# A two-layer gated-recurrence and attention block: who copies the keys of a new head pair into the working place

## What is computed

```python
q, i_in, f_fw, f_bw, z = jnp.split(h @ w_in, 5, axis=-1)
k_d = (1.0 - lbd) * jax.nn.sigmoid(-g_d)       # keys, for d = forward, backward
f_d = lbd + (1 - lbd) * jax.nn.sigmoid(g_d)    # forget gates (lbd is 0 for a single layer)
# chunk by chunk, per head:
o_inter = (q * cumulative_f) @ S
scores  = sum_k q[t] * decay[t, s] * k[s]
S_new   = diag(f_total) * S + (k * decay).T @ v
# then o = o_forward + o_backward, an RMS norm over each head, times silu(z), times w_out
```

## Time and profile before

| | |
|---|---|
| median of 3 runs | 2602.09 us (2599.35 to 2602.85) |
| the profiled execution itself | 2599.4 us, of which the span of the engines is 2597.6 us |
| TensorE busy | 2508.6 us, 97% of the span |
| VectorE, ScalarE, GpSimd busy | 1203.8, 608.2 and 263.4 us |
| mean granted TensorE clock | 0.99 of full |

### The profile page before, as it was taken

The page is one execution under the profiler, slowest core; times in us unless marked ns, Lnnn a source line. Parts: engine busy times, 40 slices in busy tenths (PEclk is TensorE's granted clock), DMA queues, the critical chain, the costliest instruction groups (busy, mean ns, idle before and its releaser), DMA issues.

```text
span 2597.6 us, 33413 instructions
## 1 busy us (share of the span) xinstructions
PE 2508.6 (97%) x13400; PEld 1959.5 (75%) x13400; DVE 1203.8 (46%) x2083; ACT 608.2 (23%) x1202; POOL 263.4 (10%) x194
## 2 busy tenths in 40 slices
PE   7999999999999999899999999999999999999999
PEld 3688888888887587666886444788886687889998
DVE  3277686696696412344136111146664014115961
ACT  3132323233232121233225100121111023113211
POOL 0012111111021100000000000111220000003310
PEclk9999999999999999999999999999999999999999
DMA  9453343343433223112520222322342232354562
GB/s 354 161 179 130 113 161 132 126 145 114 140 119 114 90 64 114 47 40 75 142 69 1 65 65 65 98 81 82 85 122 67 67 81 65 98 176 132 163 180 64
DMA packets 320030, 284.83 MB, mean 110 GB/s; under 512 B 27649, under 2 KB 298633, under 8 KB 319545
## 3 DMA queue, kind: packets, MB, share of 16 engines
q1 hardware_dynamic: 318170, 279.08, 34.7%
q0 software_dynamic: 1280, 4.20, 0.4%
q10 hardware_dynamic: 479, 0.13, 0.0%
HBM read 280.24 MB, written 3.15 MB: 109 GB/s over the span
## 4 chain that ended last, share of the span: by engine, by line
PE 82%; DVE 11%; issue 3%; ACT 3%; DMA 1%; SPq 0%; DVEq 0%; ACTq 0%
PE ps L1358 11%; PE ps L1287 10%; PE ps L721 8%; PE ps L1437 4%; PE ps L781 4%; PE ps L1425 4%; PE ps L1325 3%; PE ps L1299 3%; PE ps L819 3%; PE ps L772 2%; PE ps L905 2%; PE ps L976 2%; PE ps L925 2%; DVE arena L2317 2%; PE ps L484 2%
## 5 line engine op out<-in xcount | busy, mean ns | idle before, releaser
L1287 PE MATMUL ps<-hT,ring_mem 128*128 128x512 f32 (+1 forms) x768 | 250.3, 486 | 0.0
L1287 PEld LDWEIGHTS ps<-hT,ring_mem 128*128 128x128 f32 x768 | 145.9, 190 | 101.3 <-issue 91.4
L2248 DVE TENSOR_TENSOR arena<-ps,arena 128x512 f32<-128x512 f32 (+1 forms) x48 | 26.8, 558 | 291.2 <-PE ps L1299 291.2
L721 PE MATMUL ps<-xT,ring_mem 128*128 128x256 f32 x672 | 159.3, 380 | 0.1
L721 PE MATMUL ps<-hT,ring_mem 128*128 128x256 f32 x672 | 158.8, 379 | 0.0
L721 PEld LDWEIGHTS ps<-xT,ring_mem 128*128 128x128 f32 x672 | 127.2, 190 | 19.4 <-DVE ring_mem L2014 2.1
L819 PE MATMUL ps<-arena,K_c 128*128 128x128 f32 x896 | 120.6, 289 | 21.0 <-ACT K_c L1630 20.1
L721 PEld LDWEIGHTS ps<-hT,ring_mem 128*128 128x128 f32 x672 | 126.1, 190 | 18.9 <-issue 2.9
L1358 PE MATMUL ps<-hT,arena 128*128 128x256 f32 (+1 forms) x704 | 132.6, 333 | 7.0 <-ACT hT L505 7.0
L819 PEld LDWEIGHTS ps<-arena,K_c 128*128 128x128 f32 x896 | 115.9, 194 | 30.1 <-ACT K_c L1630 12.3
L1358 PE MATMUL ps<-arena 128*128 128x256 f32 (+1 forms) x704 | 130.0, 328 | 0.0
(11 more groups left out here) (307 smaller groups left out, 4334.4 us busy)
## 6 DMA issues: line engine op xcount, KB each, us to landing
ring_mem<-in_w_mod_dram SPq DMA_DIRECT2D x24, 2048.0 KB, 7.6
ring_mem<-in_w_up_dram SPq DMA_DIRECT2D x88, 512.0 KB, 5.1
ring_mem<-in_hg_w_in_dram SPq DMA_DIRECT2D x40, 1024.0 KB, 5.2
ring_mem<-in_w_in_dram SPq DMA_DIRECT2D x30, 1024.0 KB, 5.4
ring_mem<-in_w_down_dram SPq DMA_DIRECT2D x16, 1408.0 KB, 7.1
ring_mem<-in_ada_w_dram SPq DMA_DIRECT2D x8, 2048.0 KB, 7.6
ring_mem<-in_mla_w_in_dram SPq DMA_DIRECT2D x9, 1024.0 KB, 5.3
ring_mem<-in_hg_w_out_dram SPq DMA_DIRECT2D x8, 1024.0 KB, 12.2
```

What stands on the lines that cost most here:

```text
L721: mm = PE.matmul(dst, left[:, k, :], right[:, k, :], start=k == 0, stop=k == 3)
L1287: mm = PE.matmul(ps[:, j, 0:n], wj[:, k, m * 128:m * 128 + 128], hT[:, k, c0:T], start=k == 0, stop=k == 7)
```

## The change

The two copies `Kw <- k_st` leave VectorE and become two ScalarE copies, in a new helper that ScalarE calls behind the squares of each turn, and for pair 0 behind the last of the ten steps, ahead of the loop. A new semaphore `k_kept` counts them. VectorE's `k_sum` now waits for it.

```diff
-        kc_ready = sem("kc_ready")
+        kc_ready, k_kept = sem("kc_ready"), sem("k_kept")
...
+        def hg_unpack_scalar(act, i):
+
+            if not (isinstance(i, int) and i == 0):
+                act.wait_ge(o_full, raised(i * 2))
+            act.wait_ge(act_freed, i * 6 + 4)
+            for d in range(2):
+                S.activation(Kw[:, d * PC:d * PC + PC], k_st[:, 1 - d, :], ACT.Copy).then_inc(k_kept, 1)
...
                 hg_square_scalar(act, i - 1)
+                hg_unpack_scalar(act, i)
                 if more:
                     hg_one_scalar(act, i + 1, 0)
                     hg_seven_scalar(act, i + 1, 0)
                 hg_mean_scalar(act, i - 1)
+            hg_unpack_scalar(act, 0)
             hg_one_scalar(act, 1, 0)
             hg_seven_scalar(act, 1, 0)
...
             V.tensor_tensor(view(Qw, (PC, 2), (1, PC)), view(q_st, (0, 2), (1, PC)), f_st, ALU.mult)
-            V.tensor_copy(Kw[:, 0:PC], k_st[:, 1, :])
-            V.tensor_copy(Kw[:, PC:2 * PC], k_st[:, 0, :])
             if not first:
                 dve.wait_ge(ms_full, i * 2)
+            dve.wait_ge(k_kept, i * 2 + 2)
             V.tensor_tensor(k_sum, k_st[:, 0, :], k_st[:, 1, :], ALU.add).then_inc(unpacked, 1)
```

## The result

The changed kernel takes 2608.14 us (median of 8 runs, 2604.43 to 2612.88), the kernel before 2600.73 us (8 runs, 2599.09 to 2602.85). The ratio is 1.0027, with a 95% interval of 1.0019 to 1.0036: slower by 7.4 us in the medians. The execution that was profiled is one of the quick ones, 2604.5 us with a span of 2602.7 us, against 2599.4 and 2597.6 us in the profile of before.

A forecast was written before the change was run, and what follows sets the result against it. TensorE, 82% of the chain, was taken as the bound, so only its product starts count. Hole +4.5, clock +2.1 and pair 7 -0.4 raise the median from 2602.1 to 2608.3 us; range 2602.5 to 2611.5.

The forecast's parts named there:

- No gain at pairs 1 to 6: Boundaries of pairs 1 to 6: `k_sum` ends some 3.1 us earlier, but nobody takes it up; gain 0.
- Rival 2: Six boundaries: `K_c` comes earlier with `k_sum`, giving back 0.59 us before L819 each; +2.6 in all, 2604.7 us; chance 0.08.
- Gain at pair 7: Pair 7, without next-pair products: TensorE's 0.29 us idle before L816 goes; gain 0.4 us (0.3 to 0.5).
- The hole at the opening: Opening: late ScalarE copies hold `k_sum` and the sums behind it, delaying pair 1's product seven; TensorE hole of 4.5 us.
- The clock behind the hole: TensorE after the opening's hole: granted clock falls to half, costing 2.1 us (1.6 to 2.8).
- Rival 1: Opening: the hole opens but the clock stays at full; +4.1 us, 2606.2 us; chance 0.08.
- Rivals 3 and 4: 3: opening isn't held, -0.4, 2601.7 us, chance 0.07; 4: ScalarE's copies over 3.0 us delay product one, 2611 us, chance 0.05.
- The sum: Whole kernel: hole +4.5, clock +2.1, pair 7 -0.4, so +6.2 us and a median of 2608.3 us, 0.24% slower.
- within 0.2%: Whole kernel: chance 0.32 that the time stays within 0.2% (5.2 us) of the kernel before.

The follow-up runs named there:

- e6_kc_early: Changed kernel with pair 0's copies ahead of the value keeps and each pair's first `K_c` right behind ScalarE's key copies: 2595.62 us, ratio 0.9984 to the kernel before.
- e2: Changed kernel with only its opening kept, VectorE making the copies at the seven boundaries as before: 2607.55 us, ratio 1.0024 to the kernel before.
- e5: Changed kernel with VectorE making pair 1's first two sums ahead of pair 0's unpacking: 2603.87 us, ratio 1.0010 to the kernel before.
- e4: Changed kernel with GpSimd starting its first move only after pair 1's first sums: 2607.97 us, ratio 1.0026 to the kernel before.
- e3b: Changed kernel with ten unread products of 256 columns on TensorE ahead of pair 1's first product: 2607.40 us, ratio 1.0024 to the kernel before.

## Why the prediction was right

The median forecast was 2608.3 us, the measured one 2608.1. The way there was not as exact: the forecast stood on 2602.1 us for the kernel before, from three runs, where eight runs give 2600.7, and on a loss of 6.2 us, where the medians give 7.4. The two errors cancel. The steps, one by one:

- *No gain at pairs 1 to 6*: right. The copies took 2.00 us (forecast 2.1), `k_sum` ended 3.2 us ahead of L816 with nobody waiting, the turns that end at pairs 2 to 6 changed by at most 0.04 us each, and L819's idle time stayed, released by `K_c`. Rival 2 (`K_c` follows `k_sum`) is out. Its price was misread: the 0.59 us were counted at six boundaries, and the old trace has them at four (pairs 2 to 5), 0.72 us at pair 1 released by VectorE (L1960), and none at pair 6, so it could have given back 3.1 us at most. This did not enter the sum. `e6_kc_early` shows from the other side that `K_c` hung on ScalarE's own order.
- *Gain at pair 7*: right in place and size. The turn that ends at pair 7 is 0.51 us shorter (97.15 instead of 97.66), the others together 0.06; 0.57 in all instead of 0.4.
- *The hole at the opening*: right, 4.5 us, with every step of it: copies until 118.4, `k_sum` behind GpSimd until 120.5, sums at 121.9 in the time of the old trace. `e2` shows that it is the whole loss, `e5` that the queue behind `k_sum` makes it, `e4` that 0.9 us of it are `k_sum`'s wait for GpSimd's copy. The Trainium skill's rule on the two engines' shared reads (SBUF — State Buffer, "Who interferes with whom") was borne out by `e4`: 2.09 us beside the copy, 1.23 without it.
- *The clock behind the hole*: right in kind, a little too large, 1.8 us by the profile and 1.7 by `e3b` instead of 2.1. Rival 1 (the clock stays) came true in `e4`, at a hole of 3.44 us. The row that the price was taken from is not quite alike: behind its 4.82 us the clock was at half before TensorE went on at 845.34, as this stretch of the kernel before shows, while at the opening it fell 1 us after.

```profile
842.00:843.00 1.00, 0.00 (x0) 0.00 (x0) 1.00 (x2) 0.00 (x0) 0.00 (x0) 0.89 0.00 0
843.00:844.00 1.00, 0.00 (x0) 0.00 (x0) 1.00 (x2) 0.00 (x0) 0.00 (x0) 0.50 0.00 0
```

- *Rivals 3 and 4*: out. The opening is held, and the copies are quick.
- *The sum*: opening and pairs give +5.7 us by the table, the profiles +5.1, the medians +7.4. The forecast of +6.2 lies between, since a rest with a spread of 5 us stands in both measurements. What the forecast lacked is this: it took head and rest as fixed between the two kernels. That the median was met to 0.2 us is luck. (In the chances, the 0.32 for "within 0.2%" take in 0.03 of rival 3's 0.07, less than half and not most of it.) The changed kernel's runs spread over 8.4 us, those of the kernel before over 3.8.

## What to carry to other kernels

Where a step is moved to another engine, look at its first occurrence, outside the loop, and not only at the steady state: there the receiving engine's program order put it behind two waits that had nothing to do with it, and what cost was not the step but what stood queued behind the wait for it. An engine's long row is worth shortening only where somebody waits for its end; here the wait next door, for `K_c`, was on the receiving engine itself, and reordering that engine gave 3 us without the move and 5 with it. Where a change is worth a few microseconds, cut the spans at common starts and compare the pieces: opening and pairs repeated to 0.1 us while the whole wandered by 5.

## What the runs showed of the hardware

The same instructions, from pair 7's term 0 to the end, took between 1774.8 and 1779.9 us in fourteen profiles, each with a mean granted clock between 0.988 and 0.992. What differed, in the places compared, was which of the short idle times of TensorE were followed by a fall of the clock, and how late it rose again. An idle time of 1.90 us was followed by one in four of eight profiles and cost 1.7 us, one of 1.61 us in none of six. One of 3.44 us at the opening was not followed by any, while one of 3.60 us elsewhere was the earlier trace rows, and one of 3.10 us ahead of L1358 was in the kernel before and was not, at 3.09 us, in the changed one. The one of 4.30 us was in all three profiles that have it, and the fall came 0.9 to 1.0 us after TensorE had gone on. So whether a hole between 1.9 and 3.4 us costs the clock as well is not settled by its length.

A second fact is `k_sum` beside GpSimd: the same VectorE instruction, with two inputs in SBUF, took 2.09 us where GpSimd's copy had started 0.02 us before it, and 1.23 us in `e4_pool_later`, where GpSimd stood still. ScalarE's two copies took 2.00 us beside GpSimd's at pair 2, and 1.99 us in `e4_pool_later` with GpSimd still.
